# Prefix sums of log decays in two rounded parts, with two-pass instead of full f32 products, in the recurrences of a hybrid streaming encoder

## The reference

```
# gated DeltaNet, per head; g is a scalar log decay for each token and head
gcum  = cumsum(g)
decay = exp(where(causal, gcum_i - gcum_j, -inf))          # all pairs of a chunk
a     = where(strict, (k*beta) @ k.T * decay, 0);  solve (I + a) u = ...
o     = (q * exp(gcum)) @ s + ((q @ k.T) * decay) @ v_new
s     = s * exp(glast) + (k * exp(glast - gcum)).T @ v_new
# GLA; gk is a log decay for each token, head and key column
b     = cumsum(gk)
s     = s * exp(blast) + (k * exp(blast - b)).T @ v
```

## Time and profile before

| | |
|---|---|
| median of 3 runs | 3708.3 us (3695.61 to 3708.96) |
| the profiled execution's own time | 3698.18 us |
| its span in the profile | 3696.5 us |
| PE, PEld busy | 91%, 85% of the span |
| DVE, POOL, ACT busy | 35%, 30%, 20% |
| mean granted TensorE clock | 0.93 of full speed |

### The profile page before, as it was taken

How to read it: one execution, slowest core, us unless ns; L and a number is a source line. 1 busy time by engine, 2 the same in 40 slices (tenths; PEclk the granted TensorE clock), 3 DMA queues, 4 the chain that set the end, 5 groups by cost and what they waited for, 6 DMA issues and landing times. The chain is left out here.

```text
span 3696.5 us, 63238 instructions
## 1 busy us (share of the span) xinstructions
PE 3358.9 (91%) x26808; PEld 3140.3 (85%) x26808; DVE 1285.8 (35%) x1705; ACT 728.4 (20%) x1292; POOL 1107.2 (30%) x701
## 2 busy tenths in 40 slices
PE   5979968888658999999998997899988999999997
PEld 5968847777558999999998996666678999999997
DVE  3630033555455333333333110055532333333333
ACT  4321131232122100000101100166622000000003
POOL 4442032443061332223224233011133323232223
PEclk7989966888779999999999998899999999999999
DMA  4222120110151111111110223365611111111101
GB/s 152 85 85 93 48 64 22 42 36 34 33 187 46 46 36 55 40 40 34 41 50 12 84 93 124 114 176 146 170 44 46 46 51 40 40 34 46 51 28 51
DMA packets 269354, 246.41 MB, mean 67 GB/s; under 512 B 23624, under 2 KB 234145, under 8 KB 269176
## 3 DMA queue, kind: packets, MB, share of 16 engines
q1 hardware_dynamic: 262040, 217.49, 18.6%
q0 software_dynamic: 7136, 26.35, 2.4%
HBM read 191.77 MB, written 54.13 MB: 67 GB/s over the span
## 5 line engine op out<-in xcount | busy, mean ns | idle before, releaser
L285 PE MATMUL PS<-hT_high,w_split_tiles 128*128 128x384 f32 x5376 | 1088.1, 336 | 16.4 <-POOL w_split_tiles L299 11.0
L285 PEld LDWEIGHTS PS<-hT_high,w_split_tiles 128*128 128x128 f32 x5376 | 949.6, 189 | 16.8 <-POOL w_split_tiles L299 11.2
L285 PE MATMUL PS<-hT_low,w_split_tiles 128*128 128x384 f32 x2688 | 613.1, 335 | 0.0
L285 PE MATMUL PS<-ffn_act_split,w_down_split 128*128 128x384 f32 x3024 | 530.1, 335 | 4.9 <-issue 4.9
L285 PEld LDWEIGHTS PS<-ffn_act_split,w_down_split 128*128 128x128 f32 x3024 | 526.8, 188 | 5.2 <-issue 5.2
L285 PEld LDWEIGHTS PS<-hT_low,w_split_tiles 128*128 128x128 f32 x2688 | 482.0, 189 | 0.0
L690 DVE TENSOR_TENSOR xT<-xT,PS 128x1152 f32<-128x1152 f32 x168 | 227.4, 1354 | 300.9 <-PE PS L285 300.9
L271 PE MATMUL PS<-w_rest_split,hT_high 128*128 128x512 f32 x576 | 177.4, 389 | 0.0
L466 POOL CAST w_split_tiles<-w_raw_tiles 128x1024 fp32r<-128x1024 f32 x44 | 47.0, 1067 | 391.5 <-PE PS L285 321.3
L466 POOL CAST w_split_tiles<-attention_oT 128x1024 fp32r<-128x1024 f32 x42 | 43.7, 1041 | 342.0 <-PE PS L285 333.2
L285 PE MATMUL PS<-hT_high,w_conv_split 128*128 128x384 f32 x576 | 125.0, 343 | 4.8 <-issue 4.8
(11 more groups left out here) (398 smaller groups left out, 4803.2 us busy)
## 6 DMA issues: line engine op xcount, KB each, us to landing
w_raw_tiles<-in_ffn_w_gu_dram SPq DMA_DIRECT2D x44, 512.0 KB, 3.9
attention_oT<-in_ffn_w_gu_dram SPq DMA_DIRECT2D x44, 512.0 KB, 3.8
cache_k<-in_cache_c_k_dram SPq DMA_DIRECT2D x64, 256.0 KB, 5.6
cache_v<-in_cache_c_v_dram SPq DMA_DIRECT2D x64, 256.0 KB, 5.0
ffn_room<-in_ffn_w_down_dram SPq DMA_DIRECT2D x11, 1024.0 KB, 5.9
attention_oT<-in_ffn_w_down_dram SPq DMA_DIRECT2D x11, 1024.0 KB, 5.9
rest_dram<-rest_rows SPq DMA_DIRECT2D x36, 256.0 KB, 2.1
qk_dram<-qk_cols SPq DMA_DIRECT2D x16, 576.0 KB, 2.8
```

The lines of the kernel that those rows point to most:

```text
L285: m = nc.tensor.matmul(PS[:, banks + j, 0:GN], wl if p == 2 else wh, sl if p == 1 else sh, start=(n == 0 and p == 0), stop=(n == last and ...
```

## The change

The two kinds of sums are made the way the GLA's level sums are made already: the log decays are split into a part rounded to fp32r and the rest, and each sum is two products of fp32r operands, added up in PSUM.

- `gds` holds the DeltaNet's log decays of all nine tiles in two parts, made by two small POOL instructions ahead of `spread(0)`.
- `spread` writes `ug` for both parts: four instructions instead of two, with fp32r output.
- `spr` grows by the two matrices `after`, with two more casts on DVE ahead of `spans_put`. PE's wait for `spans_put` moves from `exponents(0)` to `dec_sums(0)`.
- `dec_sums` issues four fp32r products instead of two f32 ones; the GLA's sums are two fp32r products instead of one f32, with a wait for `gs_split`.

```diff
-        ug = e.sb(ctx, "upto_g", [P, H, P])
+        ug = e.sb(ctx, "upto_g", [P, 2, H, P], F32R)
+        gds = e.sb(ctx, "g_split", [P, 2, NT, H], F32R)
-        spr = e.sb(ctx, "spans_r", [P, 7 * P + 2 * P], F32R)
+        spr = e.sb(ctx, "spans_r", [P, 11 * P], F32R)
...
             def spread(k):
                 upto = c("upto_s" if sample(k) else "upto_p")
-                g = col(e.gdn, k)
                 dec_sum.wait(pool, k - 1)
-                for r in range(2):
-                    x = tt_(ug[:, 4 * r:4 * r + 4], over_heads(upto, 4),
-                            wide(g.rearrange("p (m r) -> p r m", r=2)[:, r], P), ALU.mult)
+                for part in range(2):
+                    g = col(gds[:, part], k)
+                    for r in range(2):
+                        x = tt_(ug[:, part, 4 * r:4 * r + 4], over_heads(upto, 4),
+                                wide(g.rearrange("p (m r) -> p r m", r=2)[:, r], P), ALU.mult)
                 x.then_inc(ug_ready.sem, 1)
...
+            nc.gpsimd.tensor_copy(gds[:, 0], e.gdn[:]).then_inc(gd_high, 1)
+            pool.wait_ge(gd_high, 1)
+            tt_(gds[:, 1], e.gdn[:], gds[:, 0], ALU.subtract).then_inc(gd_low, 1)
+            pool.wait_ge(gd_low, 1)
             spread(0)
...
+            def after_r(k):
+                return spr[:, 10 * P:11 * P] if sample(k) else spr[:, 9 * P:10 * P]
             def dec_sums(k):
-                after = c("after_s" if sample(k) else "after_p")
                 ug_ready.wait(pe, k)
                 pt_ready.wait(pe, k - 1)
+                if k == 0:
+                    pe.wait_ge(spans_put, 1)
                 for g in range(2):
-                    x = mm(PS[:, 1 + g, :], after, ug[:, 4 * g:4 * g + 4].rearrange("p h t -> p (h t)"), start=True, stop=True)
+                    for part in range(2):
+                        x = mm(PS[:, 1 + g, :], after_r(k), ug[:, part, 4 * g:4 * g + 4].rearrange("p h t -> p (h t)"),
+                               start=(part == 0), stop=(part == 1))
                 x.then_inc(dec_sum.sem, 1)
...
-                mm(PS[:, 3, 256:512], after, e.ggla[:, order[k]], start=True, stop=True).then_inc(small_mm.sem, 1)
+                gs_split.wait(pe, k)
+                for part in range(2):
+                    x = mm(PS[:, 3, 256:512], after_r(k), gsr[:, k % 2, part], start=(part == 0), stop=(part == 1))
+                x.then_inc(small_mm.sem, 1)
...
             def exponents(k):
-                if k == 0:
-                    pe.wait_ge(spans_put, 1)
...
             v.tensor_copy(spr[:, 7 * P:8 * P], c("upto_p"))
-            v.tensor_copy(spr[:, 8 * P:9 * P], c("upto_s")).then_inc(spans_put, 1)
+            v.tensor_copy(spr[:, 8 * P:9 * P], c("upto_s"))
+            v.tensor_copy(spr[:, 9 * P:10 * P], c("after_p"))
+            v.tensor_copy(spr[:, 10 * P:11 * P], c("after_s")).then_inc(spans_put, 1)
```

More of the change, by code:

```diff
@@ L1371, in recurrences @@
         states_in, states_out, zeroed, spans_put = e.sem(ctx, "states_in", "states_out", "zeroed", "spans_put")
-        ga_half = e.sem(ctx, "gla_pairs_half_put")
+        ga_half, gd_high, gd_low = e.sem(ctx, "gla_pairs_half_put", "g_high", "g_low")
         o_out = e.sem(ctx, "o_out0", "o_out1")
```

## The result

The changed kernel takes 3724.9 us in the median of 14 runs (3712.8 to 3732.2), the kernel before 3704.9 us in the median of 14 runs on the same chips (3688.2 to 3715.9). The ratio is 1.0056, 95% interval 1.0042 to 1.0070: 20 us slower. The forecast was 3709 us, within 0.5% of before. The range (3694 to 3727) holds the time, but what happened is the case to which I gave 0.14, the clock rival.

What follows compares the result with a forecast made beforehand. No engine's share bounds the kernel; DVE's chain sets the later turns, a PE-ACT chain the stage's start. Opening +6.7 us and 8 x 0 for the turns, on the 3702.8 us mean, gave 3709 us; range 3694 to 3727.

Steps and rivals of the forecast that it cites:

- the clock rival: Later turns: PE's longer stop lowers its clock, 3 us in each, 18 in six, time 3727 us; chance 0.14.
- The opening: Stage start: first pair sum waits for DVE's casts (`spans_put`), delaying the whole stage by 6.7 us (3.6 to 9).
- PE's saving: PE's sums in each turn: pair sums 0.8 us less, GLA's sums 0.25 less, together 1.0 us.
- Its idle time grows from 1.2 to 2.2 us, and the gain is 0.: PE's stop in the eight turns: PE arrives 1.0 us earlier, DVE's chain still ends the stop, so gain 0.
- One or two turns may pay and the others not.: Argument against the lower clock: a turn that lost 3 us meets the stop at another moment.
- POOL's spread, 0: Later turns: the spread's extra 2 to 3 us go into POOL's idle time, costing 0.
- POOL against DVE, 0: Later turns: DVE beside the longer spread takes data from PSUM and isn't delayed; 0, at most 8 x 1.0 us.
- PE's time counts after all: Rival for the turns: PE carries them, so up to 8 us come back, time 3701 us; chance 0.16.
- The sum: Whole kernel: 6.7 us for the opening and 8 x 0, added to the mean of four runs, 3702.8: 3709 us.

Runs made afterwards that it cites:

- moved_before: Kernel before, with PE's `outputs(s)` moved ahead of `z_blocks(i, 2)`, into PE's stop: 3687.0 us, ratio 0.9973.
- half_sums: Kernel before, with the second of the two pair-sum products left out from the second tile on: 3721.8 us, ratio 1.0068.
- spread_twice: Kernel before, with POOL's spread of the log decays written twice: 3699.3 us, ratio 1.0004.
- filler: Changed kernel, with the four pair-sum products issued twice from the second tile on: 3709.3 us, ratio 1.0036 to the kernel before.
- early_casts: Changed kernel, with DVE's five casts of the 0/1 matrices ahead of its five memsets: 3718.6 us, ratio 1.0065 to the kernel before.
- the moved kernels: `outputs(s)` ahead of `z_blocks(i, 2)` in the kernel before, the changed one, and the changed one with casts before memsets: ratios 0.9973, 0.9985, 0.9976.
- moved_after: Changed kernel, with PE's `outputs(s)` moved ahead of `z_blocks(i, 2)`: 3692.2 us, ratio 0.9985 to the kernel before.

## Why the prediction was right in its range and wrong in its case

- *The opening, +6.7 us (3.6 to 9).* Measured 7.7 us at L1600/L1616 and 7.9 at the first inverse. `spans_put` decided, as said: 506.78 against an assumed 507.3. The way there was different in part. The first casts stood beside POOL's spread, not beside the multiplications after it, and the spreads took 6.64 us instead of 4.1. All of that is in the fourth, of 3.64 us (row below); the three ahead of it took 1.04 each, beside DVE's memsets. Of the short casts one took 1.05 us and the last 0.75. By the Trainium skill (SBUF — State Buffer, section "Who interferes with whom") either side can be the one that waits, whichever issues second. Here POOL lost more than DVE, although its fourth spread starts 2.2 us ahead of the first cast, which that order doesn't explain. All transposes ran at 1.2 GHz, where I had allowed for half; moved_before shows that this happens without the change too, so part of the 7.9 us is not the change's.

```profile
501.76 3.64 POOL L1488 TENSOR_TENSOR upto_g<-consts_r,g_split 128x512 fp32r<-128x512 f32 x1
```

- *PE's saving, 1.0 us per turn.* Right: the stops grew from 1.2 to 2.2 us.
- *"Its idle time grows from 1.2 to 2.2 us, and the gain is 0."* This is the step that failed. There is indeed no gain, since DVE's chain ends when it did; but the longer stop had a consequence. The rows for it were in the trace of before, and the rival was priced from them at 3 us per turn and 18 in all. Measured: 16.6 us in eight turns with five falls. My reason against it was that the dense L1769 stands ahead of the stop. It stood there in all five. I had also read from one turn that the clock stays at 1.00 behind a stop of 1.20 us; in the same trace it fell behind another such stop, at 670 us:

```profile
670.50:680.00 9.50, 9.50 (x159) 0.50 0.05 20
```

- *"One or two turns may pay and the others not."* Wrong in number: the clock fell in five of six, and in six in half_sums. That a later turn meets the stop at another moment is true, and it didn't protect it.
- *POOL's spread, 0, and POOL against DVE, 0.* Right, by spread_twice and by filler.
- *PE's time counts after all.* Wrong while the stop is there; it begins to show once the stop is filled.
- *The sum.* 3709 was 6.7 us on the mean of four runs. The 14 runs of before have a median of 3704.9, and 3709.5 + 16.6 would be 3726, which is 1 us from the measured 3724.9. That the range holds this time is owed to its upper end, which took in the full price of the rival; the forecast's own bounds, 3699 to 3718, miss it.

## What to carry to other kernels

In this kernel, work taken off PE ahead of a step at which it waits anyway gained nothing and cost time: the idle time grew, and what followed ran at half the clock. Before shortening PE's work ahead of such a wait, look how long PE will then stand, and whether elsewhere in the same trace a stop of that length is followed by a granted clock of 0.50; if it is, first fill the stop with work that doesn't depend on what it waits for. Here that move alone was worth 0.27%, more than the 8 us (0.2%) that the change takes off PE. A profile is one execution, and the clock differs between executions and kernels even where nothing was changed, so a difference of a few us read from two profiles needs the timed runs beside it.

## What the runs showed of the hardware that was not expected

- Between a stop of 1.2 to 1.3 us and one of 2.1 to 2.2 us, in otherwise the same turn, falls of the clock go from 1 in 6 (before, filler, spread_twice) to 5 or 6 in 6 (changed, early_casts, half_sums); at 1.7 us it was 2 in 6, and at stops below 0.5 us 1 in 18 (the moved kernels). Each count is from one profiled execution. Each fall left PE at 1.2 GHz for at least 6 to 13 us in the changed kernel's rows above, and for some 3 us in moved_after.
- One POOL instruction of the opening took 3.64 us (501.76 to 505.40), where three of the same form ahead of it took 1.04. It overlapped DVE's last memset (502.26 to 504.03) and the cast of 896 columns behind it (503.95 to 504.51). The kernel before has the same at this place: L1498 took 2.68 us (502.48 to 505.16) and L1499 behind it 1.04. In early_casts, where no cast stands behind the memset, POOL's instructions beside it took 1.04 each. In spread_twice, where the same memset and cast stand together again, POOL's cast of 128x256 took 2.74 us (0.39 elsewhere). So it isn't the memset alone; in all three a POOL instruction that started ahead of the cast and overlapped the memset ended only behind the cast. Why, no run here shows.
- A cast of 128 columns took 0.21 us where it began in the gap between two POOL instructions (505.74), and 1.06 and 1.08 us beside POOL's spread in early_casts.
